# A chained two-block kernel: two input-projection panels start before the mixers' keys, the mixers stand 5.4 blocks apart, and eight ada row chunks move to the output projection

## The reference

```python
mod = c_act @ ada_w[layer] + ada_b[layer]
sh1, sc1, g1, sh2, sc2, g2 = [m[:, None, :] for m in jnp.split(mod, 6, axis=-1)]
u = rms_norm(h, norm_mix_g[layer]) * (1.0 + sc1) + sh1
h = h + g1 * hybrid_mixer(u, w_in[layer], ..., w_out[layer])
u = rms_norm(h, norm_ffn_g[layer]) * (1.0 + sc2) + sh2
h = h + g2 * swiglu(u, w_gate, w_up, w_down)
```

## Time and profile before

| what | value |
|---|---|
| median of 3 runs | 2101.37 us (2100.27 to 2101.46) |
| the profiled execution, its own time | 2103.02 us |
| its span, first to last instruction | 2101.3 us |
| mean granted PE clock | 0.996 |
| PE / DVE / ACT busy | 98% / 68% / 50% |

### The profile page before, as it was taken

How to read it: one execution, slowest core, us unless ns; L and a number is a source line. 1 busy time by engine, 2 the same in 40 slices (tenths; PEclk the granted TensorE clock), 3 DMA queues, 4 the chain that set the end, 5 groups by cost and what they waited for, 6 DMA issues and landing times.

```text
span 2101.3 us, 28591 instructions
## 1 busy us (share of the span) xinstructions
PE 2065.6 (98%) x9829; PEld 1701.9 (81%) x9829; DVE 1426.9 (68%) x2490; ACT 1060.4 (50%) x1969; POOL 89.2 (4%) x159
## 2 busy tenths in 40 slices
PE   7999999999999999999999999999999999999998
PEld 5787788888877888888888888888888788888886
DVE  6987899899588885555555556854465755555566
ACT  3544555556454544445444444554454555555552
POOL 1001011010004000000000000000000000000000
PEclk9999999999999999999999999999999999999999
DMA  9999889888658886666666665564466455555563
GB/s 335 368 371 314 280 293 301 284 287 284 210 171 275 288 288 218 192 190 190 190 190 194 190 189 189 190 234 140 149 197 216 157 162 179 172 161 170 180 225 116
DMA packets 281609, 468.87 MB, mean 223 GB/s; under 512 B 17136, under 2 KB 111568, under 8 KB 280080
## 3 DMA queue, kind: packets, MB, share of 16 engines
q1 hardware_dynamic: 278416, 451.22, 66.0%
q0 software_dynamic: 2768, 15.98, 2.3%
q10 hardware_dynamic: 304, 0.10, 0.0%
HBM read 465.13 MB, written 2.10 MB: 222 GB/s over the span
## 4 chain that ended last, share of the span: by engine, by line
PE 93%; DVE 5%; DMA 1%; issue 1%; ACT 0%; DVEq 0%; ACTq 0%; POOL 0%; POOLq 0%
PE ps L588 82%; PE ps L910 1%; DVE w_lo L533 1%; PE ps L882 1%; DVE acc_a L513 1%; PE ps L1789 1%; PE ps L1110 1%; PE ps L1088 1%; DVE acc_b L513 1%; PE ps L564 1%; PE ps L894 1%; DMA X<-in_x 1%; PE ps L1691 0%; DVE ada_acc L545 0%; PE ps L1775 0%
## 5 line engine op out<-in xcount | busy, mean ns | idle before, releaser
L533 DVE TENSOR_TENSOR w_lo<-raw,w_hi 128x512 fp32r<-128x512 f32 (+2 forms) x1264 | 859.6, 691 | 590.0 <-ACT w_hi L485 585.7
L485 ACT ACTIVATE w_hi<-raw 128x512 fp32r<-128x512 f32 (+2 forms) x1264 | 787.7, 629 | 868.0 <-PE ps L588 837.2
L588 PE MATMUL ps<-w_hi,actT 128*128 128x512 f32 (+2 forms) x3712 | 1012.8, 394 | 0.0
L588 PEld LDWEIGHTS ps<-w_hi,actT 128*128 128x128 f32 x3712 | 686.2, 188 | 144.5 <-issue 10.2
L588 PE MATMUL ps<-w_lo,actT 128*128 128x512 f32 (+2 forms) x1856 | 572.0, 389 | 3.9 <-DVE w_lo L533 3.8
L588 PEld LDWEIGHTS ps<-w_lo,actT 128*128 128x128 f32 x1856 | 348.0, 188 | 79.8 <-DVE w_lo L533 6.7
L588 PE MATMUL ps<-w_hi,hidT 128*128 128x512 f32 x704 | 189.6, 391 | 0.0
L588 PEld LDWEIGHTS ps<-w_hi,hidT 128*128 128x128 f32 x704 | 131.4, 188 | 27.5 <-issue 0.5
L588 PE MATMUL ps<-w_lo,hidT 128*128 128x512 f32 x352 | 108.6, 390 | 0.5 <-DVE w_lo L533 0.5
L588 PE MATMUL ps<-w_hi,mixT 128*128 128x512 f32 x384 | 104.3, 390 | 0.0
L513 DVE SCALAR_TENSOR_TENSOR acc_a<-raw,c_col,acc_a 128x1024 f32<-128x1024 f32 x75 | 97.7, 1302 | 1.7
(11 more groups left out here) (309 smaller groups left out, 1559.0 us busy)
## 6 DMA issues: line engine op xcount, KB each, us to landing
raw<-in_w_in SPq DMA_DIRECT2D x208, 512.0 KB, 4.7
raw<-in_ada_w SPq DMA_DIRECT2D x192, 512.0 KB, 5.4
raw<-in_w_out SPq DMA_DIRECT2D x96, 512.0 KB, 3.9
raw<-in_ffn_w_gate SPq DMA_DIRECT2D x176, 256.0 KB, 2.9
raw<-in_ffn_w_up SPq DMA_DIRECT2D x176, 256.0 KB, 3.2
raw<-in_ffn_w_down SPq DMA_DIRECT2D x88, 512.0 KB, 4.2
raw<-in_w_kv_shared SPq DMA_DIRECT2D x48, 512.0 KB, 3.7
raw<-in_w_mem_kv SPq DMA_DIRECT2D x32, 512.0 KB, 6.7
```

The costliest lines, as they stand in the source:

```text
L485: act.activation(half(p, at_p, it.g + b, 0, w), raw[:, slot_of(st, it), b, 0:w], ACT.Copy).then_inc(hi_ready, 1)
L533: nc.vector.tensor_tensor(half(p, at_p, it.g + b, 1, w), raw[:, slot, b, 0:w], half(p, at_p, it.g + b, 0, w).bitcast(f32), ALU.subtract).t ...
L588: last = nc.tensor.matmul(ps[:, bank_of(st, it.j) + t, 0:w], lhs[:, int(which == 1), kk, t * P:(t + 1) * P], half(p, at_p, it.g + b, int(w ...
```

## The change

- `win_k` gets two more panels in front, the first two of `win` (columns 2880 to 3903): 8 w items, chunks 0 to 3 of both, one A item behind each. They gather in the banks that panels 2 and 3 of the stage use after them; ACT copies the half sums out (`take_early`). Then come the three key panels, one A item behind each w item up to chunk 4, one w item, the nine A items left, and the last 8 w items.
- `win` now has only chunks 4 to 7 of these two panels: 64 w items, 128 blocks, numbered from 16 (`n0=16`). DVE adds their sums to the half sums (`add_early`, at blocks 30 and 38); ACT skips them.
- The duos stand at 27 + (130 i + 12) // 24, that is 5 or 6 blocks apart, from 27 to 157. The other steps beside the mixers are renumbered.
- A items: 80 in `win` (two behind every fourth w item, now in the last panel too), 16 in `wout`, behind its w items 4 to 19 (blocks 152 to 183), not 8 behind its items 0 to 7.
- The dummy matmuls of `sum_and_run` go, those of `last_sum` are 6, not 14. `k_twice` and `w1` move by some bytes.

The diff, cut to its core:

```diff
     for ch in range(4):
-        for j in range(3):
+        for j in range(2):
             weights(j, ch)
             ada()
+    for ch in range(5):
+        for j in range(2, 5):
+            weights(j, ch)
+            ada()
+    weights(2, 5)
+    while a:
         ada()
-    ada()
-    ada()
-    for j in range(3):
-        weights(j, 4)
-        ada()
-    weights(0, 5)
-    for _ in range(11):
-        ada()
-    weights(1, 5)
-    weights(2, 5)
+    weights(3, 5)
+    weights(4, 5)
     for ch in range(6, 8):
-        for j in range(3):
+        for j in range(2, 5):
             weights(j, ch)
...
-        if n < 8:
-            order.append(("A", 0, 8 + n, 1))
+        if 4 <= n < 20:
+            order.append(("A", 0, n - 4, 1))
...
-    for m in range(72):
-        order.append(("w", m // 8, m % 8, 0))
-        for _ in range(2 if m < 64 and m % 4 == 3 else 1):
+    weights = [(j, ch) for j in range(9) for ch in range(4 if j < 2 else 0, 8)]
+    for m, (j, ch) in enumerate(weights):
+        order.append(("w", j, ch, 0))
+        for _ in range(2 if m % 4 == 3 else 1):
...
-    Stage("memkv", 1, [("wA", 16)] * 4), Stage("win_k", 1, [("w", 16)] * 3, k_major(), banks=(0, 2, 4)),
-    Stage("win", 1, [("w", 16)] * 9, win_order(), an_given=4),
+    Stage("memkv", 1, [("wA", 16)] * 4), Stage("win_k", 1, [("w", 16)] * 5, k_major(), banks=(0, 2, 0, 2, 4)),
+    Stage("win", 1, [("w", 16)] * 9, win_order(), an_given=4, n0=16),
...
-        DUO_AT = [13 + 6 * i for i in range(len(DUOS))]
+        DUO_AT = [27 + (130 * i + 12) // 24 for i in range(len(DUOS))]
...
+            def last_sum():
                 pe.wait_ge(S("dist"), 1)
                 between_sums(3, 6)
-
-            def last_sum():
-                between_sums(3, 14)
                 ada_sum(pe, st_k, 0, 1, True)
...
+                    if j < skip:
+                        return
+                    if skip and j == skip:
+                        act.wait_ge(acc_read, 2 + At(st, p).pn + skip)
...
+            def take_early(j):
+                panel_done(act, st_k, 0, j)
+                for t in range(T):
+                    last = a.activation(proj[:, t, WIN[j]:WIN[j] + NC], ps[:, bank_of(st_k, j) + t, :], ACT.Copy)
+                last.then_inc(acc_read, 1)
...
+            def add_early(j):
+
+                st = ST["win"]
+                dve.wait_ge(acc_read, 2 + st.start[2] + j)
+                panel_done(dve, st, 0, j)
+                for t in range(T):
+                    part = proj[:, t, WIN[j]:WIN[j] + NC]
+                    last = v.tensor_tensor(part, part, ps[:, bank_of(st, j) + t, :], ALU.add)
+                last.then_inc(acc_read, 1)
```

More of the change, by code:

```diff
@@ L1247, in _ @@
                                                ("w", 0, 5): lambda: mem_quarter(3)})
[L1248 removed]
+            stage_loads(sp, "win_k", lambda p, j, ch: [((0, NC), blocks2(w_in[0], 0, ch, FIRST_K[j], NC))], ada_pair(0, 2))
             second = ada_pair(1, 0)
@@ L1824, in stage_copy @@
             def stage_copy(name, dst, flag=None, width=None, lead=None, hooks={}, func=(ACT.Copy, ACT.Copy), defer=False,
-                           at=None, scaled=False, each=None):
+                           at=None, scaled=False, each=None, skip=0):
                 st = ST[name]
                 def take(p, j):
+                    if j < skip:
+                        return
+                    if skip and j == skip:
+                        act.wait_ge(acc_read, 2 + At(st, p).pn + skip)
                     panel_done(act, st, p, j)
@@ L1991, in _ @@
             take_win = stage_copy("win", lambda p, j, t: proj[:, t, WIN[j]:WIN[j] + WIN_W[j]], width=WIN_W,
-                                  lead={0: lambda: take_k(0), 2: lambda: take_k(1), 5: lambda: take_k(2)}, defer=True,
-                                  each=beside_mixer)
+                                  lead={8: lambda: take_k(0), 10: lambda: take_k(1), 13: lambda: take_k(2)}, defer=True,
+                                  each=beside_mixer, skip=2)
             stage_split_hi(act, "wout", each=beside_mixer)
@@ L2201, in fox_start @@
             def fox_start():
-                dve.wait_ge(acc_read, 2 + ST["win_k"].start[2] + 1)
+                dve.wait_ge(acc_read, 2 + ST["win_k"].start[2] + 3)
                 dve.wait_ge(S("cmp_in"), 16 * 6)
@@ L2352, in beside_mixer @@
             def beside_mixer(n):
-                if n == 7:
+                if n == 23:
                     fox_start()
-                elif n == 6:
+                elif n == 22:
                     cmp_positions()
-                elif n == 8:
+                elif n == 24:
                     lambda_dots()
-                elif n == 20:
+                elif n == 30:
+                    add_early(0)
+                elif n == 36:
                     cmp_take()
-                elif n == 21:
+                elif n == 37:
                     first_gates()
-                elif n == 26:
+                elif n == 38:
+                    add_early(1)
+                elif n == 42:
                     fox_ratio()
-                elif n == 28:
+                elif n == 46:
                     lambda_end()
-                elif n in (30, 33):
-                    far(*((2, 3), (3, 15))[(n - 30) // 3])
-                elif n == 38:
+                elif n in (47, 50):
+                    far(*((2, 3), (3, 15))[(n - 47) // 3])
+                elif n == 54:
                     fox_terms((15, 13, 11, 9))
-                elif n == 46:
+                elif n == 60:
                     fox_terms((7, 5, 3))
-                elif n == 52:
+                elif n == 64:
                     fox_log()
-                elif n in (32, 58, 84, 111):
-                    take_pair(4 + (32, 58, 84, 111).index(n))
-                elif n == 103:
+                elif n in (48, 74, 100, 125):
+                    take_pair(4 + (48, 74, 100, 125).index(n))
+                elif n == 110:
                     dilated_lse()
-                elif n == 109:
+                elif n == 116:
                     dilated_weights()
-                elif n == 127:
+                elif n == 131:
                     subnorm_squares()
-                elif n == 132:
+                elif n == 136:
                     subnorm_scale()
```

67 lines of the change are left out of this document (35 added, 32 removed).

## The result

The kernel before took 2100.96 us (median of 20 runs, 2099.2 to 2102.16), the changed kernel **2105.51 us** (median of 20, 2102.26 to 2107.38). The ratio is 1.0022, with a 95% interval of 1.0016 to 1.0028: 4.5 us slower, where the forecast had 5.1 us faster. The profiled execution of the changed kernel has a span of 2101.8 us and a time of 2103.54, so it is one of the quicker ones of its kind; the span before was 2101.3.

A forecast was written before the change was run, and what follows sets the result against it. The prediction took PE, busy 98% of the span, as the bound, with transfers in the head and DVE as edges. Terms -21.8 + 11.3 + 1.2 + 2.9 + 1.3 gave -5.1 us: 2096.3 us, range 2090.0 to 2105.0.

The forecast's parts named there:

- Eight items, -21.8 us: In `win`: eight w items, 96 matmuls, leave PE's path, saving 21.8 us.
- Head +11.3 us: In `win_k`: eight more items at the transfers' pace of 1.417 us each delay the last sum by 11.3 us.
- the head is PE's: Rival, chance 0.03: in the head PE loses its 7.5 us in hand waiting for u's pieces; each further us is paid.
- Additions +1.2: At blocks 30 and 38: four DVE additions from PSUM cost PE 1.2 us, bounds 0 and 2.4.
- Mixers every 5.4 blocks, +2.9: In the mixers: reordered steps make `scores` wait for the copy, 2.9 us in all, bounds 0 and 8.
- PE's own work stays: In the mixers: the same 25 duos, so no added PE work at the new spacing.
- Turn behind `normed`, 0: In the mixers: `normed` stands later before `turn`, but a stalled PE lets DVE get ahead; cost 0.
- The rival counted nine of 1.6 us: Rival, chance 0.12: `turn` waits for `normed` in nine cases, 14.6 us, giving 2110.9 us.
- Narrow panel +1.3: In the narrow panel: ten A items instead of eight, where DVE bounds, cost net 1.3 us, bounds 0 and 3.
- Clock as before, 0: Behind the head's last sum: the same 1.7 us clock loss as before despite a longer wait; added cost 0.
- A items in `wout`: In `wout`, blocks 152 to 183: sixteen A items, twelve of them new there, cost 0.
- nothing is given back: Rival, chance 0.18: additions, copies and narrow panel lose nothing more; -21.8 + 11.3, giving 2090.9 us.

The follow-up runs named there:

- best version: Changed kernel with late mixer steps and maxima one block earlier, 12 filler matmuls, and six instead of ten A items beside the narrow panel: 2090.57 us.
- 17 fillers: Kernel before, with 17 instead of 14 filler matmuls in front of the last sum of its head: 2100.03 us against 2100.72.
- The changed kernel again: The changed kernel as it is, measured a second time: 2106.29 us, ratio 1.0028.
- twelve fillers: Changed kernel with 12 instead of 6 filler matmuls ahead of the last sum of the head: 2102.02 us.
- no additions: Changed kernel without the four DVE additions of `add_early`, their wait and signal kept: 2104.40 us.
- three handovers: Changed kernel with exponentials, turn of probabilities and copy of mixers 6, 11, 18 and maxima of 7, 12, 19 one block earlier: 2102.86 us.
- normed alone: Changed kernel with only VectorE's statistics and normed output of each mixer one block earlier: 2110.41 us.

## Why the prediction was wrong

It gave half of the chance to a gain and 0.16 to a loss of this size. The work saved came as forecast; what failed are four terms, of which the sum had two at nothing (steps that no longer share a block, 3.5 us, and the clock, some 2.5) and two too low (waits, 7.5 us for 5.4, and the head, 12.2 for 11.3). Of its steps:

1. *Eight items, -21.8 us: right.* Sixteen blocks at 1.36 us left; the best version, with 0.7 us of waits, has the busy time of 340.4 us that this leaves (340.8).

2. *Head +11.3 us: too low.* It took 12.2 us, and 13.4 against the head of before in the profile with 17 fillers, which has no fall of the clock in it. PE was there when forecast: its real work ended 70.8 us after the first sum (114.25 to 185.05), against 70.7 worked out. The step that failed is the conclusion drawn from it: the forecast compared the sums at the end, 188.0 and 195.5, and called the difference 7.5 us in hand. But PE has nothing in hand in the middle. The chain lies on PE up to 179.3 us, buffers come free at PE's pace, and the transfers fall to 339 GB/s, which is not made up later. A likely reason lies in the order, though no run tests it: before, the first four chunks had four A items for three w items, now there is one behind each, a pair takes PE 2.72 us and the transfers 2.83, and any sum or turn on PE then holds up the stream. The rival "the head is PE's" named the right engine, but neither how (PE had no gap, and did not wait for u's pieces) nor the price, 1 to 2 us.

3. *Additions +1.2: right*, by the 1.1 us of idle time that went without them; the medians alone (1.1 us) don't show it.

4. *Mixers every 5.4 blocks, +2.9: the mechanism right, the list too short.* The three handovers came as worked out (2.8 us of waits in all, and 2.6 us by the medians when they were taken away). That their sum meets the +2.9 is in part luck: the forecast counted two of them and nine waits of 0.1 us, and there were all three, and three of 0.08 to 0.09 us. What failed is the sentence "PE's own work stays", the largest single term, 3.5 us put at nothing. Its instructions stay; but before, a turn of probabilities shared a step with a turn, and outputs with scores, and a step apart costs the block behind it 0.1 to 0.15 us. The busy time stood 3.5 us above 340.8, and fell to 339.3 when the steps were put together again. The forecast had even noted the "0.1 more behind transposes", and did not multiply it.

5. *Turn behind `normed`, 0: too low.* Four waits of 0.5 to 1.2 us, 3.9 in all. Three of them needed the load of the narrow panel (they went with it), and the one at 274 us, where the forget-gate step stood in front of `normed`, went with the additions of item 3. The rival counted nine of 1.6 us; DVE does get ahead again after each, as the forecast said against it.

6. *Narrow panel +1.3: too low.* Moving four A items out of it took 4.0 us of waits away and 5.8 us of time, more than the waits; how much of the rest is the clock's is open. DVE was taken at its busy time over the whole of the stretch; the balance of sixteen narrow blocks alone, 4.6 us of DVE to 3.8 of PE in every four, was never made.

7. *Clock as before, 0: too low, by some 2.5 us.* With the wait of 4.23 us the stretch at 1.2 GHz around the sum lasted 10.2 us in the first profile, 8.3 of them from the sum on, and 6.8 us in seven others, against 3.4 before. In the first profile that is (8.3 - 3.4) / 2 = 2.4 us more, and by the medians about 2.5, worked out under "The changed kernel again". The two are not wholly the same loss: the runs' mean holds falls in the mixers too. The Trainium skill (TensorE: Matmul & The Clock Gate, HAM oscillation — how this bites in real kernels) puts such losses down to idle gaps between bursts of matmuls. The trace agrees for the long gap: 12 fillers in it gave 3.5 us. It doesn't for the fall with only 0.34 us of waiting in front of it, nor for those at 281.5 to 284.4 us in four profiles (the first one, twelve fillers, no additions, three handovers), where the last wait was over 9 us back or there was none.

The sum for the profiled execution: -21.8 + 12.2 (head) + 7.5 (waits, 9.2 less the 1.7 of before) + 3.5 (steps apart) + 2.4 (clock behind the sum) = +3.8, against 3.6 us measured. Against the forecast's -5.1 that is 0.9 more for the head, 2.1 for the waits (7.5 for 1.2 + 2.9 + 1.3), 3.5 for the steps apart and 2.4 for the clock. A items in `wout` cost nothing, as forecast: from the fillers on, and in the 80 us before them but for the outputs of one mixer that slid across the mark (1.4 us), nothing is longer. The best version, 2090.57, comes out where the "nothing is given back" case stands (2090.9), in part by luck: its head is as much too dear as that of the changed kernel, and its mixers wait 0.7 us where the kernel before waited 1.7.

What stays open: why the clock falls at one short wait and not at the same wait in another execution, why it falls in places without a wait, and why it fell with 17 fillers. No run here separates the wait from the sum's own sixteen matmuls of one column. That is the rival left standing: the falls at 281.5 to 284.4 us all began 1.2 to 1.8 us behind the end of such a sum, and so did, at 1.1 and 1.3 us, those at 336.1 (twelve fillers) and 341.2 us (normed alone); in the narrow panel there is no sum near. What the early panels alone are worth, with the old spacing, was not tried.

## What to carry to other kernels

When work is taken out from between steps that are timed against each other in blocks, list for each pair of steps that shared a place where each now stands, in each engine's order, and move the whole set by one if that puts them together again; here this was worth 8.9 us, more than the change's own forecast. Moving one engine's part alone can make it worse. Slack that is worked out at the end of a stage is no slack for a transfer stream that is held up in its middle by buffers that come free too late. And a long wait can cost the clock besides itself: judge a version by the times and the mean granted clock of many runs, since one profile shows one draw.

## What the runs showed that was not expected

- A block behind a small step is 0.1 to 0.15 us longer (1.17 to 1.20 us for its first four matmuls against 1.07), so the number of places at which steps interrupt blocks has a price of its own, 3.5 us here.
- A wait of the same length in the same place (0.99 us, scores of mixer 8) had a stretch at 1.2 GHz beginning in it in one execution and not in another. Mean granted clock over the runs: 0.9942 changed, 0.9965 before, 0.9970 in the best version.
- PE's wait for a DVE step can be put down to "issue" in the groups; DVE's timeline at that time shows the step it waited for.
